# Operand tiles of the 256-token phases packed 512 columns apart, in a fp32 encoder kernel on one core

## The reference

```
h = concatenate([meta, x])                                  # 272 x 2048
h = h + even_mixer(rms_norm(h, g), w_in, w_out, ...)        # layer 0: 2048 -> 3072, 2048 -> 2048
h = h + square(relu(rms_norm(h, g) @ w1)) @ w2              # 2048 -> 8192 -> 2048
h = h + (B * dwconv3(C * h_in)) @ w_out                     # layer 1: [B | C | h_in] = rms_norm(h, g) @ w_in, 2048 -> 6144
h = h + square(relu(rms_norm(h, g) @ w1)) @ w2
return rms_norm(h, g)[:, 16:]                               # 256 x 2048
```

## Time and profile before

| | us |
|---|---|
| median of 3 runs | 2115.35 (2115.12 to 2116.29) |
| profiled execution, its own time | 2116.13 |
| profiled execution, span from its first to its last instruction | 2114.1 |
| TensorE matmuls busy | 2089.6 |
| TensorE weight loads busy | 1985.3 |
| VectorE busy | 1281.1 |
| ScalarE busy | 927.1 |
| DMA | 383.91 MB, 182 GB/s on the mean |

### The profile page before, as it was taken

One profiled execution on the slowest core, in us unless ns is written; L12 is line 12 of the kernel. 1 busy time (PEld: TensorE's weight loads), 2 busy tenths in 40 slices (PEclk: granted clock), 3 DMA queues, 4 the chain that ended last, 5 costly groups with the idle time before them and its releaser, 6 DMA issues.

```text
span 2114.1 us, 36370 instructions
## 1 busy us (share of the span) xinstructions
PE 2089.6 (99%) x15226; PEld 1985.3 (94%) x15226; DVE 1281.1 (61%) x1300; ACT 927.1 (44%) x965; POOL 66.1 (3%) x40
## 2 busy tenths in 40 slices
PE   8999999999999999999999999999999999999997
PEld 8999999999999999999999999888888888888886
DVE  8999975545554554556566556665556555555555
ACT  6434464334434443445433334545335434434443
POOL 1001020000000000000100000010000000000001
PEclk9999999999999999999999999999999999999999
DMA  7442455555555555554555455455554554554552
GB/s 283 178 160 101 162 185 192 179 181 187 188 180 179 183 189 183 179 180 177 196 183 179 179 189 189 168 202 187 187 191 179 198 181 178 197 188 178 193 195 80
DMA packets 55336, 383.91 MB, mean 182 GB/s; under 512 B 6176, under 2 KB 8224, under 8 KB 9312
## 3 DMA queue, kind: packets, MB, share of 16 engines
q1 hardware_dynamic: 54880, 381.84, 50.1%
q0 software_dynamic: 240, 1.02, 0.1%
q10 hardware_dynamic: 144, 0.04, 0.0%
HBM read 380.78 MB, written 2.10 MB: 181 GB/s over the span
## 4 chain that ended last, share of the span: by engine, by line
PE 96%; DVE 2%; ACT 1%; issue 0%; DMA 0%; DVEq 0%; SPq 0%
PE banks L310 25%; PE banks L304 20%; PE banks L302 19%; PE banks L303 19%; PE banks L311 13%; DVE wl L796 1%; ACT wh L519 0%; DVE h L824 0%; ACT xs L536 0%; DMA raw<-weights 0%; DVE ssum L935 0%; DVE h L1149 0%; DVE h L1155 0%; ACT sq L546 0%; PE banks L437 0%
## 5 line engine op out<-in xcount | busy, mean ns | idle before, releaser
L796 DVE TENSOR_TENSOR wl<-raw,wh 128x1024 fp32r<-128x1024 f32 x720 | 891.9, 1249 | 720.6 <-ACT wh L519 719.5
L519 ACT ACTIVATE wh<-raw 128x1024 fp32r<-128x1024 f32 x720 | 753.9, 1058 | 971.3 <-PE banks L304 610.9
L302 PE MATMUL banks<-xs,wh 128*128 128x258 f32 (+1 forms) x2176 | 618.3, 284 | 10.3 <-DVE wl L796 10.3
L304 PE MATMUL banks<-xs,wl 128*128 128x258 f32 (+1 forms) x2176 | 621.1, 285 | 0.0
L303 PE MATMUL banks<-xs,wh 128*128 128x258 f32 (+1 forms) x2176 | 614.3, 282 | 0.0
L310 PE MATMUL banks<-hid,wh 128*128 128x512 f32 x1280 | 448.5, 395 | 0.0
L302 PEld LDWEIGHTS banks<-xs,wh 128*128 128x128 f32 x2176 | 412.4, 190 | 10.6 <-issue 8.8
L303 PEld LDWEIGHTS banks<-xs,wh 128*128 128x128 f32 x2176 | 411.4, 189 | 0.1
L304 PEld LDWEIGHTS banks<-xs,wl 128*128 128x128 f32 x2176 | 409.9, 188 | 0.0
L304 PE MATMUL banks<-hid,wl 128*128 128x258 f32 x1280 | 363.8, 284 | 0.0
L302 PE MATMUL banks<-hid,wh 128*128 128x258 f32 x1280 | 361.9, 283 | 1.4 <-DVE hid L840 1.4
(11 more groups left out here) (103 smaller groups left out, 779.5 us busy)
## 6 DMA issues: line engine op xcount, KB each, us to landing
raw<-weights SPq DMA_DIRECT2D x359, 1024.0 KB, 4.8
out<-h SPq DMA_DIRECT2D x8, 256.0 KB, 2.7
h<-x SPq DMA_DIRECT2D x3, 544.0 KB, 10.6
raw<-weights SPq DMA_DIRECT2D x2, 512.0 KB, 6.0
conv<-dft_seq POOLq DMA_DIRECT2D x1, 580.5 KB, 13.2
h<-x SPq DMA_DIRECT2D x2, 272.0 KB, 4.3
act<-dft_ch POOLq DMA_DIRECT2D x1, 258.0 KB, 7.9
par<-params POOLq DMA_DIRECT2D x1, 160.0 KB, 6.4
```

What stands on the lines that cost most here:

```text
L302: pe.matmul(dst, w[0], v[0], start=start, stop=False)
L304: return pe.matmul(dst, w[1], v[0], start=False, stop=stop)
L519: act.activation(wh[:, j % RING, :, :], src.rearrange("p (t c) -> p t c", t=SLAB_K), ACT.Copy).then_inc(high_ready, 1)
L796: dve.tensor_tensor(wl[:, j % RING, :, :], src.rearrange("p (t c) -> p t c", t=SLAB_K), wh[:, j % RING, :, :].bitcast(F32), ALU.subtract). ...
```

## The change

Nothing is added to or taken from the instructions. Only where the parts of `xs` and `hid` stand differs, and only in calls with `lo == FROM2`, the phases of 256 tokens. There, a second view lies over the same memory, with tiles of 512 columns (2048 bytes) in place of 544 (2176 bytes). High parts are columns 0 to 255 of a tile and low parts columns 256 to 511. With `lo` of 0 or 14 the places are as before.

```
+        packed = {id(t): t[:, :, :].rearrange("p k l -> p (k l)")[:, 0:KT * COLS]
+                  .rearrange("p (k l) -> p k l", k=KT) for t in (xs, hid)}
+
         def high_of(t, tile, lo):
-            return t[:, tile, lo:L]
+            return packed[id(t)][:, tile, 0:N2] if lo == FROM2 else t[:, tile, lo:L]
 
         def low_of_tile(t, tile, lo):
-            return t[:, tile, L:2 * L - lo]
+            return packed[id(t)][:, tile, N2:2 * N2] if lo == FROM2 else t[:, tile, L:2 * L - lo]
 
         def both_of(t, tile, lo):
-            return t[:, tile, lo:2 * L - lo]
+            return packed[id(t)][:, tile, 0:2 * N2]
```

## The result

The median of 11 runs of the changed kernel is 2109.79 us (2109.01 to 2122.71), against 2116.21 us (2115.07 to 2116.39, 11 runs) for the kernel before: a ratio of 0.9977, 95% interval 0.9969 to 0.9984. It is faster by 6.4 us, where no change was forecast.

A forecast was written before the change was run, and what follows sets the result against it. The prediction took TensorE's matmul stream to bound the 256-token part. Its three terms, operand start, even and odd tiles, and writers, summed 0 + 0 + 0, giving 2115.4 us, the median of the runs shown; range 2107.5 to 2123 us.

The forecast's parts named there:

- What bounds it: 256-token part: TensorE's own matmul stream is the bound, busy the whole 807.1 us; only the time between matmul starts matters.
- Price of a pair: 256-token part: 2304 pairs of a wide and a narrow matmul, so 1 ns a pair is 2.3 us.
- the plain rhythm: 256-token part: undisturbed pairs at 350.1 ns make 806.6 of 807.2 us; some 0.6 us is loop turns and the norm's matmul.
- Part one, the start of the moving operand: Wide and narrow matmuls: new starts of their moving tiles change nothing, 0 taken, at most 3.2 us in all.
- the DFT rows: Sequence DFT: matmuls from scattered starts take 120.1 ns against 119.4 for regular ones, bounding the start's effect at 0.7 ns.
- Part two, even and odd tiles: Wide matmuls alternate 0.40 and 0.39 us by tile; weights or banks can carry that, so 0 taken, +/-5.8 us for range.
- the sign: Changed profile: if wide matmuls no longer alternate, the alternation was one of the moving operand's starts, otherwise of weights or banks.
- the three readings: Even and odd wide tiles: a shift lent and given back, free to lose; or all pairs take the longer form; or the shorter.
- Part three, the writers: ScalarE and VectorE writing tiles at a step of 512 columns: under 0.3 us, hidden by TensorE, so 0.
- Rival B: 256-token pairs: the alternation itself costs, so like tiles run in the shorter form; -5.8 us, 2109.6 us; chance 0.17.
- Rival A: 256-token pairs: the low half of a 256-byte block is the dearer start; +5.8 us, 2121.2 us; chance 0.26.
- Rival C: 256-token pairs: the 30 ns over 320 pay for crossing a larger boundary and go; 69 us less, 2046 us; chance 0.05.

The follow-up runs named there:

- places: TensorE alone, 19 segments of 128 pairs or triples with other operand places; layout of before 350.0 ns a pair, changed layout 353.3 and 346.8.
- seeded: The changed kernel with hid 32 bytes further on in the second mixer's output projection (256 pairs); median 2109.08 us, ratio 0.9983 to the kernel before.
- places2: TensorE alone, 24 segments: tiles 2048 bytes apart at starts of 0 to 240 bytes, and 258-column triples; 346.7 to 353.4 ns a pair.
- weights64: The changed kernel with both weight rings 64 bytes further on; median 2128.53 us, ratio 1.0057 to the kernel before.
- history: TensorE alone, 24 segments of 64 to 384 pairs or triples; the changed layout seven times, mostly behind different streams: about 346.7 or 353.3 ns a pair.
- again: The changed kernel once more, unaltered, for another trace; median 2110.56 us, ratio 0.9982 to the kernel before.

## Why the prediction was wrong

**What bounds it: right.** TensorE's stream alone sets the time of the 256-token part; its length moved with ns per pair times 2304 and, by under 1 us, with the interruptions. VectorE, ScalarE and the DMAs play no part, as places shows.

**Price of a pair: right.** The unit of 2.3 us per ns carries the results: 350.0 - 346.7 = 3.3 ns makes 7.7 us. Seeded's profiled execution lies 7.7 us under before's, 2116.13 - 2108.46, of which 7.1 us stand in the 256-token part (800.1 against 807.2 us) and the rest ahead of it. The surplus over the plain rhythm was read a little wrong: with 350.0 ns a pair it is 0.8 us, half of it the norm's matmul and half three waits for low weights. Loop turns show no gap.

**Part one, the start of the moving operand, "I take 0": the first step that failed.** The bound of 0.7 ns a matmul, 3.2 us in all, came from the DFT rows, a mean over starts that change from matmul to matmul. A mean over mixed starts says nothing of a repeated one. Places2 gives 346.7 to 353.4 ns for uniform starts, 6.7 ns between them, 15 us of the kernel. And I looked only at the moving operand; the other half of the distance, the weights' own place, did not enter at all.

The Trainium skill, "SBUF — State Buffer", section "Who interferes with whom", gives TensorE two independent read ports, one for the moving operand and one for weight loads, and says that it never waits on anyone. The measurements do not agree if it is read to mean that these two reads leave each other alone: in places, moving the weights alone by 64 or 128 bytes turned the pace and the inner pattern of start 0 into those of 192 and 128, and in weights64 no execution took less than 2127.38 us, where the changed kernel has nearly all at 2110 (4.6 us of this are in the 258-column triples). The same page's note on 16-byte lines, weighed in the prediction, has no room for 353.3 against 346.7 ns between starts of 192 and 32 bytes, both on a line.

**Part two, even and odd tiles, "I take 0, as these can carry the alternation alone": the step that decided the sign.** The alternation was the moving operand's: with equal starts it vanished, which the prediction named as the sign. Of the three readings, "a shift that one tile lends and the next gives back" is half right: 353 and 347 are the two halves of one pattern of 700 ns and neither is a price, for given to all tiles, both starts cost 353.3 (start 64 once 348.9, in history). But its removal was not free: "I take 0" stood for a change of 3.3 ns a pair, down to 346.7 in the fast pace of start 0 and up to 353.3 in the slow one. The size, 2.5 ns, was estimated from rounding.

**Part three, the writers: right.** ScalarE and VectorE have the busy times of before, 362.4 and 463.5 us in the part.

**Rivals.** Rival B is what happened in most executions: a stream whose tiles look alike can run in a shorter form, forecast at 2109.6 against a median of 2109.79. Its direction was right, and its size, 5.8 us, near the 6.4 measured. That the two times agree to 0.2 us is luck: 2.5 ns came from rounding and the fast pace is 3.3 ns under before's, while the kernel before had 2116.21 us in this comparison and not 2115.4; its reason (a start off step waits for the next slot) is at best incomplete, since other uniform starts are slower. Rival A has the size of the executions in the 353.3-ns rhythm, 2121.2 against 2122.7, but not its reason: start 192, in the upper half, is as slow as 64. Rival C, the boundary, is refuted by start 32, which beats start 0. I gave B 0.17 and A 0.26 because two shapes seemed to speak for A; the 258-column rows spoke neither way and I had no third shape.

**What stays open.** The step that failed is known, and so is what stood in its place; the cause within the chip is not. Open are what makes a pattern repeat, which of two paces a stream takes at its beginning and behind an interruption, and why both profiled executions of the changed kernel but 1 of 18 ordinary ones took some 2122 us. Seeded's 3 of 11 ordinary ones may differ from that by chance. The paces of repeating patterns (346.7 for one pair, 700 for two, 1060 and 1053 for three) are all whole multiples of 6.67 ns, which is a fact of the records and not an explanation.

## What to carry to other kernels

Where TensorE has no idle time and every matmul brings its own weights, the pace depends on where the moving operand starts relative to the weights, by 2% between the uniform offsets here (fp32r, 512 and 256 columns); it is worth timing a few uniform offsets, in steps of 16 bytes, rather than arguing for the aligned one. A small stream of matmuls alone, with the kernel's own order and places, reproduces such paces to 0.1 ns, at the price of one short run for twenty layouts. It does not tell which of two paces a layout takes in the kernel: start 16 showed only 346.7 ns alone and had a stretch at 360.0 in the kernel. Prefer an offset that never showed a second pace (32 bytes here: 2107.98 to 2109.11 us in its 5 executions) over one that has two, and change both moving tensors, `xs` and `hid`, together: half of this change was slower than none. A trace holds one execution; compare its time with the others before reading it as the usual one.

## What the runs showed of the hardware that was not expected

- One layout has two stable paces: 346.7 or 353.3 ns a pair at start 0, in the same trace, and what ran before has a hand in which. An interruption of under 0.5 us, a wait for weights or one matmul of another kind, can switch between them (again at 1392 us, seeded at 1392 and 1400 us).
- At the lower clock level a pair takes 640 ns, which is 768 columns at 1.2 GHz with nothing on top: the six pairs behind the first in places (layout of before) and in places2 (start 0). The cost on top, and with it its dependence on the places, showed at the upper level alone.
- The moving operand's distance to the weights counts, nearly always by 256 bytes alone: weights moved by 64 and 128 gave 353.3 and 351.1 ns, as did the moving operand at 192 and 128. One combination, 16 with 208, does not fit.
- No pace is near the columns' 320 ns. The Trainium skill, "TensorE: Matmul & The Clock Gate", section "Back-to-back issue gap", has 2.5 ns on top of the columns of a matmul by itself, and says that a stream in which each matmul has a weight load is paced by both; it gives no figure for fp32r. The 256-token pairs have (346.7 - 320) / 2 = 13.3 to 16.7 ns and the 258-column matmuls 11.8 to 13.6, with fp32r operands and a weight load for each matmul. So the stream does not run at the isolated gap, and the prediction's 325 ns was the wrong figure to hold against it. Whether the operand type or the weight loads make the difference was not tried.
